# A chunked two-way recurrence on one core: inverting 64x64 diagonal blocks instead of 128x128 ones, with the next step's matrices built inside this step

## What is computed

```python
def _rwkv_step(S, xs):
    r, w, k, v, kk, a = xs
    sa = jnp.einsum('bhij,bhj->bhi', S, -kk)
    S = S * w[:, :, None, :] + sa[..., None] * (kk * a)[:, :, None, :] + v[..., None] * k[:, :, None, :]
    return S, jnp.einsum('bhij,bhj->bhi', S, r)
# forward and backward:
s, ys = lax.scan(_rwkv_step, s0.astype(f32), xs, reverse=reverse)
```

## Time and profile before

| | |
|---|---|
| median of 3 runs | 3408.24 us (3405.17 to 3410.75) |
| the profiled execution | 3406.34 us, span 3404.5 us |
| TensorE passes busy | 2853.8 us (84%), x16786 |
| VectorE, ScalarE, GpSimd busy | 1727.5, 1490.8, 334.1 us |
| HBM read | 458.30 MB |

### The profile page before, as it was taken

How to read it: one execution, slowest core, us unless ns; L and a number is a source line. 1 busy time by engine, 2 the same in 40 slices (tenths; PEclk the granted TensorE clock), 3 DMA queues, 4 the chain that set the end, 5 groups by cost and what they waited for, 6 DMA issues and landing times. The chain is left out here.

```text
span 3404.5 us, 47820 instructions
## 1 busy us (share of the span) xinstructions
PE 2853.8 (84%) x16786; PEld 2435.6 (72%) x16786; DVE 1727.5 (51%) x2453; ACT 1490.8 (44%) x2103; POOL 334.1 (10%) x469
## 2 busy tenths in 40 slices
PE   4994948888998767999896968997499999999994
PEld 2971937777787256888685848885488888888883
DVE  3135634444443424332223117873288888888886
ACT  1221744433433012333112215652177777777774
POOL 0024111111200010000010003311100000000002
PEclk7996969999999887999997988998599999999997
DMA  5233010000001522221313241112299999999996
GB/s 190 78 122 111 1 45 1 1 1 1 1 1 46 190 87 81 74 74 49 101 48 99 80 150 28 28 42 76 100 345 346 343 363 342 355 355 344 358 344 225
DMA packets 306607, 479.05 MB, mean 141 GB/s; under 512 B 58336, under 2 KB 228816, under 8 KB 306224
## 3 DMA queue, kind: packets, MB, share of 16 engines
q1 hardware_dynamic: 294912, 444.77, 38.6%
q10 hardware_dynamic: 7152, 17.89, 1.4%
q0 software_dynamic: 4416, 14.70, 1.3%
HBM read 458.30 MB, written 18.98 MB: 140 GB/s over the span
## 5 line engine op out<-in xcount | busy, mean ns | idle before, releaser
L2467 DVE TENSOR_TENSOR m_lo<-m_raw,m_hi 128x1408 fp32r<-128x1408 f32 (+1 forms) x459 | 662.7, 1462 | 140.1 <-ACT m_hi L2419 136.7
L2419 ACT ACTIVATE m_hi<-m_raw 128x1408 fp32r<-128x1408 f32 (+1 forms) x459 | 567.4, 1248 | 131.0 <-PE p_ups L2370 79.2
L186 PE MATMUL acc<-w_hi,h_hi 128*128 128x512 f32 (+1 forms) x1120 | 427.0, 381 | 41.8 <-DVE w_lo L171 35.8
L171 DVE TENSOR_TENSOR w_lo<-w_raw,w_hi 128x1024 fp32r<-128x1024 f32 (+1 forms) x134 | 157.8, 1179 | 561.0 <-ACT w_hi L164 560.9
L187 PE MATMUL acc<-w_lo,h_hi 128*128 128x512 f32 (+1 forms) x1120 | 425.5, 380 | 0.0
L188 PE MATMUL acc<-w_hi,h_lo 128*128 128x512 f32 (+1 forms) x1120 | 423.9, 378 | 0.0
L164 ACT ACTIVATE w_hi<-w_raw 128x1024 fp32r<-128x1024 f32 (+1 forms) x134 | 135.6, 1013 | 516.2 <-PE acc L188 480.5
L186 PEld LDWEIGHTS acc<-w_hi,h_hi 128*128 128x128 f32 x1120 | 212.9, 190 | 78.9 <-DVE w_lo L171 37.4
L188 PEld LDWEIGHTS acc<-w_hi,h_lo 128*128 128x128 f32 x1120 | 212.7, 190 | 34.3
L187 PEld LDWEIGHTS acc<-w_lo,h_hi 128*128 128x128 f32 x1120 | 213.0, 190 | 32.7
L1813 ACT ACTIVATE a_power<-p_unit 128x512 f32<-128x512 f32 x240 | 133.2, 561 | 205.7 <-PE p_unit L1737 205.7
(11 more groups left out here) (310 smaller groups left out, 5648.8 us busy)
## 6 DMA issues: line engine op xcount, KB each, us to landing
m_raw<-moe_w_gu SPq DMA_DIRECT2D x544, 352.0 KB
m_raw<-moe_w_dn SPq DMA_DIRECT2D x187, 512.0 KB
ada_w<-ada_w SPq DMA_DIRECT2D x40, 1024.0 KB, 8.2
w_raw<-ffn_w_gu SPq DMA_DIRECT2D x88, 256.0 KB, 2.9
w_raw<-w_in_o SPq DMA_DIRECT2D x24, 512.0 KB, 3.7
w_raw<-ffn_w_dn SPq DMA_DIRECT2D x22, 512.0 KB, 3.5
w_raw<-w_in_e SPq DMA_DIRECT2D x28, 384.0 KB, 3.3
scratch_y_slots<-y_slot ACTq DMA_DIRECT2D x18, 512.0 KB, 6.3
```

What stands on the lines that cost most here:

```text
L171: eng.tensor_tensor(self.w_lo[:, part, 0:2 * self.width], self.raw[:, slot, 0:2 * self.width], self.w_hi[:, part, 0:2 * self.width], ALU.s ...
L186: eng.matmul(out, hi, whi[:, b, :], start=first, stop=False)
L2419: a.activation(whi[:, u % MSPLIT, 0:size(u)], raw[:, s, 0:size(u)], ACT.Copy).then_inc(s_hi.sem, 1)
L2467: dve.tensor_tensor(wlo[:, u % MSPLIT, 0:n], raw[:, u % MRAW, 0:n], whi[:, u % MSPLIT, 0:n], ALU.subtract).then_inc(s_lo.sem, 1)
```

## The change

The 128x128 triangular matrix A of a head is split into 64x64 blocks. Only the two diagonal blocks are inverted by squaring, now with five squarings (levels 0 to 4) and five inverse products (levels 1 to 5), each a pair of 64x64 products in the two diagonal quarters of the array. The corner block follows from them: corner_pe (slots 6 and 7) multiplies the corner of A with one diagonal inverse, turns the other inverse, and multiplies the two, with a copy by ScalarE between and one by VectorE behind. TF is cleared once, so its other corner stays zero.

A step has eight slots (SLOTS_OF_STEP). walk puts products, masks and turns of step n + 1 into slots 4 to 6 of step n; chain_r, chain_u and chain_end go behind slots 0, 1 and 3. PREP has new slots, and each of its matrix products is two pieces in slots of their own. The PSUM banks are dealt anew: powers one bank a direction, one bank for the inverse products of both directions, two for the masked products, one for all turned matrices and preparation products. wait_read makes TensorE wait, before it writes a shared bank, until the last reader is done.

```diff
-    LEVELS = 6
+    LEVELS, SLOTS_OF_STEP = 6, 8
...
-            X = K.sb(scan, "a_power", [P, 2, 2, 2, 2, P])
-            W = K.sb(scan, "inverse_so_far", [P, 2, 2, 2, P])
+            AX = K.sb(scan, "a_turned", [P, 2, 2, 2, P])
+            XW = K.sb(scan, "powers_inverse", [P, 2, 2, 2, 3, HD])
             TF = K.sb(scan, "inverse_t", [P, 2, 2, 2, P])
+            PT = K.sb(scan, "inverse_parts", [P, 2, 2, 2, HD])
...
-            pU = [K.ps(scan, f"p_unit{d}", [P, 3, 512]) for d in range(2)]
+            pA = [K.ps(scan, f"p_powers{d}", [P, 512]) for d in range(2)]
+            pI = K.ps(scan, "p_inverse", [P, 512])
+            pM = K.ps(scan, "p_products", [P, 2, 512])
+            pX = K.ps(scan, "p_turned", [P, 512])
...
+            reader = {"turned": None, "inverse": None}
+            def wait_read(pe, bank, signal, count):
+                if reader[bank] is not None:
+                    pe.wait_ge(reader[bank][0].sem, reader[bank][0].at(reader[bank][1]))
+                reader[bank] = signal, count
+            def pair_pe(pe, ct, k, i, lhs, rhs):
+                a, b = PIECES[i]
+                if k == 0:
+                    wait_read(pe, "turned", s_eps, 2 * ct + i + 1)
+                else:
+                    wait_read(pe, "turned", s_sig, 8 * ct + 2 * (k - 1) + i + 1)
+                pe.matmul(pX[:, 0:b - a], lhs, rhs[:, a:b], start=True, stop=True).then_inc(s_prod.sem, 1)
...
+            PREP = [(0, "act", squares_act)] + [(1 + i, who, f(i)) for i in range(2) for who, f in (("pe", norm_pe), ("act", norm_act))]
+            PREP += [(3, "dve", norm_dve)]
+            for d, at in ((0, 4), (1, 19)):
+                PREP += [(at + 2 * w + i, who, f(d, w, i)) for w in range(2) for i in range(2) for who, f in (("pe", lora_pe), ("act", lora_act))]
+                PREP += [(at + 2, "pool", decay_pool(d)), (at + 4, "dve", scan_dve(d)), (at + 5, "dve", centre_dve(d)),
+                         (at + 5, "pool", rate_pool(d)), (at + 6, "pool", other_pool(d)),
+                         (at + 6, "act", middle_act(d)), (at + 8, "act", exps_act(d)), (at + 11, "dve", tilde_dve(d))]
...
-                if s:
-                    pe.wait_ge(u_tt[d].sem, u_tt[d].at(LEVELS * s))
-                pX, pM = pU[d][:, 2, :], pU[d][:, 0:2, :]
-                pairs = [k for k in range(5) if PAIR_STEP[k] < i] if ct + 1 < CT else []
-                last, k = (ct + 1, pairs[-1]) if pairs else (ct, 4)
-                if k == 0:
-                    pe.wait_ge(s_eps.sem, s_eps.at(2 * last + 2))
-                else:
-                    pe.wait_ge(s_sig.sem, s_sig.at(8 * last + 2 * k))
-                pe.transpose(pX[:, 2 * P:3 * P], cols(Kt[ct % 2][d], c), K.ident[:])
-                pe.transpose(pX[:, 3 * P:4 * P], cols(Bt[ct % 2][d], c), K.ident[:]).then_inc(u_xk.sem, 1)
+                wait_read(pe, "turned", u_kb, q + 1)
+                pe.transpose(pX[:, 0:P], cols(Kt[ct % 2][d], c), K.ident[:])
+                pe.transpose(pX[:, P:2 * P], cols(Bt[ct % 2][d], c), K.ident[:]).then_inc(u_xk.sem, 1)
+                if q:
+                    pe.wait_ge(u_rest.sem, u_rest.at(2 * q))
...
+                wait_read(pe, "turned", u_x0, q + 1)
...
+            def powers_bank(d):
+                return pA[d][:, 0:2 * P].rearrange("p (h x n) -> p h x n", h=2, x=2)
+            def inverse_bank():
+                return pI[:, 0:P].rearrange("p (h n) -> p h n", h=2)
             def level_pe(pe, ct, i, d, l):
                 q, s, c, par = unit(ct, i, d)
-                pA, pI = pU[d][:, 0, :], pU[d][:, 1, :]
+                if l >= LEVELS:
+                    return corner_pe(pe, ct, i, d, l)
+                cur, out = l % 2, powers_bank(d)
+                def x(hh, b):
+                    return AX[head(b), par, d, hh, head(b)] if l == 0 else XW[head(b), cur, d, hh, 2, :]
+                def xt(hh, b):
+                    return AM[head(b), par, d, hh, head(b)] if l == 0 else XW[head(b), cur, d, hh, 0, :]
                 if l == 0:
                     pe.wait_ge(u_x0.sem, u_x0.at(q + 1))
-                    pe.wait_ge(u_rest.sem, u_rest.at(2 * q + 2))
                 else:
-                    pe.wait_ge(u_xw[d].sem, u_xw[d].at(LEVELS * s + l))
-                cur = l % 2
-                if l < LEVELS:
+                    pe.wait_ge(u_xw[d].sem, u_xw[d].at((LEVELS - 1) * s + l))
+                if l < LEVELS - 1:
                     for hh in range(2):
-                        x = X[:, cur, d, hh, 1, :]
-                        xt = AM[:, par, d, hh, 0:P] if l == 0 else X[:, cur, d, hh, 0, :]
-                        if l < LEVELS - 1:
-                            pe.matmul(pA[:, 2 * hh * P:(2 * hh + 1) * P], x, xt, start=True, stop=True)
-                        mm = pe.matmul(pA[:, (2 * hh + 1) * P:(2 * hh + 2) * P], xt, x, start=True, stop=True)
+                        if l < LEVELS - 2:
+                            for b in range(2):
+                                pe.matmul(out[head(b), hh, 0, :], x(hh, b), xt(hh, b), start=True, stop=True)
+                        for b in range(2):
+                            mm = pe.matmul(out[head(b), hh, 1, :], xt(hh, b), x(hh, b), start=True, stop=True)
                     mm.then_inc(u_sq[d].sem, 1)
                 if l:
                     if l == 1:
-                        pe.wait_ge(u_tt0.sem, u_tt0.at(q + 1))
+                        pe.wait_ge(u_tt0.sem, u_tt0.at(2 * q + 2))
                     else:
                         pe.wait_ge(u_tt[d].sem, u_tt[d].at(LEVELS * s + l - 1))
+                    wait_read(pe, "inverse", u_tt[d], LEVELS * s + l + (l == LEVELS - 1))
                     for hh in range(2):
-                        mm = pe.matmul(pI[:, hh * P:(hh + 1) * P], X[:, cur, d, hh, 1, :], W[:, cur, d, hh, :], start=True, stop=True)
+                        for b in range(2):
+                            mm = pe.matmul(inverse_bank()[head(b), hh, :], x(hh, b), XW[head(b), cur, d, hh, 1, :], start=True, stop=True)
                     mm.then_inc(u_iv[d].sem, 1)
+            def corner_pe(pe, ct, i, d, l):
+                q, s, c, par = unit(ct, i, d)
+                near, far = head(d), head(1 - d)
+                if l == LEVELS:
+                    pe.wait_ge(u_tt[d].sem, u_tt[d].at(LEVELS * (s + 1)))
+                    for hh in range(2):
+                        pe.matmul(pA[d][near, hh * HD:(hh + 1) * HD], AX[far, par, d, hh, near], TF[far, par, d, hh, far], start=True, stop=True)
+                    for hh in range(2):
+                        mm = pe.matmul(pA[d][near, P + hh * HD:P + (hh + 1) * HD], TF[:, par, d, hh, near], K.ident[:, near], start=True, stop=True)
+                    mm.then_inc(u_ab[d].sem, 1)
+                else:
+                    pe.wait_ge(u_pt[d].sem, u_pt[d].at(s + 1))
+                    wait_read(pe, "inverse", u_fin[d], s + 1)
+                    for hh in range(2):
+                        mm = pe.matmul(pI[near, hh * HD:(hh + 1) * HD], PT[near, d, 1, hh, :], PT[near, d, 0, hh, :], start=True, stop=True)
+                    mm.then_inc(u_c[d].sem, 1)
...
-                pe.wait_ge(u_tt[d].sem, u_tt[d].at(LEVELS * (s + 1)))
+                pe.wait_ge(u_fin[d].sem, u_fin[d].at(s + 1))
...
-                a.wait_ge(u_sq[d].sem, u_sq[d].at(LEVELS * s + l + 1))
-                if l:
-                    a.wait_ge(u_iv[d].sem, u_iv[d].at(LEVELS * s + l - 1))
                 if l < LEVELS - 1:
-                    out, src = X[:, (l + 1) % 2, d].rearrange("p h x n -> p (h x n)"), pU[d][:, 0, :]
-                else:
-                    out, src = X[:, (l + 1) % 2, d, :, 1, :], pU[d][:, 0, :].rearrange("p (h x n) -> p h x n", h=2, x=2)[:, :, 1, :]
-                a.activation(out, src, ACT.Copy).then_inc(u_xw[d].sem, 1)
+                    a.wait_ge(u_sq[d].sem, u_sq[d].at((LEVELS - 1) * s + l + 1))
+                    first = 0 if l < LEVELS - 2 else 1
+                    a.activation(XW[:, (l + 1) % 2, d, :, 2 * first::2, :], powers_bank(d)[:, :, first:, :], ACT.Copy).then_inc(u_xw[d].sem, 1)
+                elif l == LEVELS:
+                    near = head(d)
+                    a.wait_ge(u_ab[d].sem, u_ab[d].at(s + 1))
+                    a.activation(PT[near, d].rearrange("p x h n -> p (x h n)"), pA[d][near, 0:2 * P], ACT.Copy).then_inc(u_pt[d].sem, 1)
...
+                if l < LEVELS - 1:
+                    dve.tensor_tensor(XW[:, (l + 1) % 2, d, :, 1, :], XW[:, l % 2, d, :, 1, :], inverse_bank(), ALU.add).then_inc(u_tt[d].sem, 1)
+                elif l == LEVELS - 1:
+                    if q >= 4:
+                        dve.wait_ge(c_y.sem, c_y.at(q - 3))
+                    for b in range(2):
+                        dve.tensor_tensor(TF[head(b), par, d, :, head(b)], XW[head(b), l % 2, d, :, 1, :], inverse_bank()[head(b)],
+                                          ALU.add).then_inc(u_tt[d].sem, 1)
+                elif l == LEVELS + 1:
```

(35 more changed lines are left out.)

## The result

The changed kernel takes 3435.62 us (median of 5 runs, 3434.13 to 3448.35) against 3410.75 for the kernel before on the same chip: ratio 1.0081, 95% interval 1.006 to 1.0102. It is slower by 0.8%, where 0.9% faster was forecast. The time is inside the range given, its sign was the unlikely one. The span of the profiled execution is 3434.1 us, 29.6 longer than before.

A forecast was written before the change was run, and what follows sets the result against it. TensorE was taken to bound the recurrence. Quiet steps of 21.9 against 24.92 us save 60 us in 20 steps; preparation costs 27 and the first pair 4, leaving about 30 us faster: 3378 us, range 3330 to 3440.

The forecast's parts named there:

- Passes and their number: Levels on TensorE: 16 squaring and 8 inverse passes of 29 ns, 0.70 us a direction and level instead of 1.34.
- Rival 1: Levels: diagonal tiles take turns on one bank, 58 ns a pass, step 26.7 us, time 3465 us; chance 0.17.
- Shared bank and the wait behind the masks: Inverse products 0.93 us apart; level 5 of direction 1 waits 2.3 us behind VectorE's masks, 0.6 of it filled.
- Shape changes: TensorE switching tile shape: about 14 more changes a step, taken at 0.15 us each.
- the sum of a quiet step: TensorE's step without preparation, from one last product pass of direction 0 to the next: 21.9 us against 24.92.
- Rival 3: Quiet steps: shape changes nearly free and overlapped by waits, 28 us less, time 3350 us; chance 0.14.
- One sign: VectorE's busy share in a quiet step would rise from 10.3 in 24.9 us to half.
- rival 2: Every step: the clock falls to half for 3.4 us, costing up to 1.7 us, time 3412 us; chance 0.13.
- Preparation: Steps preparing the next pair of heads: some 9 us dearer a pair than 26.3, 27 us in three pairs.
- the second scan: Preparing steps: TensorE idle 1.8 us while VectorE's second scan stands in front of a needed addition.
- the second set of matrices: Preparing steps: TensorE idle 1.9 us while VectorE makes the second set of scaled matrices.
- The start: First pair's preparation, before the recurrence: no cover, its pieces take turns on the bank, 4 us dearer.

The follow-up runs named there:

- the wide passes in slot 6: Changed kernel, idle 1.68 us kept, with seven 128x128 products put in front of direction 0's corner products: 3425.01 us.
- among whole matrices: Kernel before, with three spare VectorE products ahead of direction 0's level 5 addition in the last five steps: 3417.55 us (544 columns), 3421.97 us (640).
- at level 3: Changed kernel with level 5 products in their direction's own bank, plus spare 640-column VectorE products ahead of direction 0's level 3 addition, last five steps: 3396.54 us.
- the order alone: Changed kernel's walk and shared banks, but whole 128x128 squarings and inverse products with seven levels as in the kernel before: 3430.77 us, ratio 1.0075.
- the blocks alone: Changed kernel's 64x64 blocks and corners, but each step's products, masks and turns at its own start as before: 3486.26 us, ratio 1.0227.

## Why the prediction was wrong

**Passes and their number: right.** 29 ns a 64x64 pass, both diagonal tiles on one bank at once (1047.38 to 1047.49). Rival 1, tiles in turn, is refuted. The two tiles lie on different rows of the array and write one bank, and here the measurement decides against the rule cited with it. They write different partitions of it, and no row shown has two row tiles on the same ones.

**Shared bank and the wait behind the masks: right.** Inverse products follow at 0.92 us (1049.53 and 1050.45) for 0.93, and the idle ahead of level 5 of direction 1 is 1.68 us for 2.3 less 0.6.

**Shape changes and the sum of a quiet step: right at full clock.** 21.9 us was forecast; the kernels whose only difference is work inside the idle have 21.83 and 21.92, where the step of before has 24.92. Rival 3 falls with it. One sign was off: VectorE is busy 9.2 us of such a step, 0.42 of it, where half was forecast. And chain_u stands in the sum with 0.90 us where its row reads 0.84.

**The clock: the step that failed.** "A quiet step of after" was summed at clock 1.00, and rival 2 priced a fall at 3.4 us of half speed a step, from the one short fall in the earlier trace rows, with a chance of 0.13. A fall came in each of the five quiet steps. In four it lasted 13.7 us and cost 5.5 us a step instead of 1.7 at most; in the fourth step it lasted 3.4 and cost 1.5, the rival's price. In the whole recurrence the granted clock is 0.77, so about 284 of 617.6 us ran at half speed; before it was 0.94, some 71 of 593. The mechanism of the rival was right, its size was off by three, and it took the place of the forecast. The price was read from one of the shortest falls of the kernel before; others there lasted 6.8 us (as 597.65 to 604.47).

The recurrence took 55 us more than forecast (617.6 against some 563). 23.5 of them are in the five quiet steps (133.0, from 972.80 to 1105.80, against 109.5), some 31 in the fifteen preparing ones. That the time lies inside the range is luck: the range reached up to 3440 to hold the case of one short fall a step, and what came were falls four times as long.

**Preparation: mis-sized, for the same reason.** Two of the idle places came as forecast, 5.23 us at the reciprocal for 5.5 and 2.98 at the first set of scaled matrices for 2.9:

```profile
849.18 0.58 PE L1763 MATMUL p_inverse<-powers_inverse 64*64 64x64 f32 x6 [5.23 <-DVE powers_inverse L1883]
...
898.32 0.55 PE L1791 MATMUL p_chain<-v_rows,a_masked 128*128 128x64 f32 x3 [2.98 <-DVE state_mid L1905]
```

Others did not: the second scan left 4.28 us (925.91 to 930.19) for 1.8, the second set of matrices no more than a quiet step has for 1.9. Their sum is near the forecast: TensorE is idle 27.0 of the 152.9 us, 14.6 more than in five slow quiet steps, for 14. But a pair's preparation costs 45.8 us over quiet steps where these run at full clock (148.60 less five of 20.57), not 35. In that kernel the clock is 0.79 over the five steps, so 31 us of full speed are missing (0.21 of 148.6); before, at 0.94 of 150.9, it was 9. The sum had left this term at what it was before. In the changed kernel itself preparation looks cheap, 152.9 against five quiet steps' 133.0, only because the quiet steps are slow too. The start was forecast 4 us dearer and is 2.7 later.

**What stays open.** That the idle 1.68 us brings the falls of the quiet steps is shown: with the wait gone, or with passes in its place, they run at clock 1.00. When an idle brings a fall, and how long it lasts, is not settled. The fourth quiet step has the same passes and the same idle as the others, and a fall of 3.4 us. In the first four the falls start 1.30, 1.21, 1.12 and 1.01 us behind the idle: they come 27.3 us apart, the steps are 27.4 us long. So the moment at which the idle comes is a rival to what stands behind it, and it was not tested: no run moves one and keeps the other. With it agrees that of five like idles only some had a fall behind them, one beside the wide passes in slot 6, two among whole matrices, two at level 3, three in the order alone. If the stretch behind the idle has a part in it, the turns are not enough, since in the order alone they follow the idle and the falls stayed at 3.4 us. And the blocks alone fall deepest with no idle over 0.84 us; whether their six short ones add up, or the passes between them count, is open.

## What to carry to other kernels

Before work on TensorE is made smaller, list the idle places that its other engines will open, and read the granted clock as a term of the sum: here 1.7 us of idle cost 6.8 in four of five quiet steps. A fall may be priced too low from the shortest one in sight. A shared PSUM bank made such a place here, because its reader stood in a queue behind other work; giving the one product that waits a bank that is free at that moment turned 0.8% slower into 0.8% faster. Cutting the element-wise pieces that stand in front of a short step gave 29 us here (3381.04 to 3352.04); do it before the step is shortened.

## What the runs showed of the hardware

- Two 64x64 tiles on the diagonal with outputs in one bank run together at 29 ns a float32 pass with 64 columns.
- Idle of 0.72 us a step: no fall. Idle of 1.40 us among whole matrices: none in three steps; 1.70: a fall of 3.4 us behind two of five. Idle of 1.68 with the products, turns and corners behind it: a fall of 13.7 us in four of five steps, clock 0.75, and of 3.4 in one, 0.93; the same with 14 wide passes 2.1 us behind it: one fall of 3.4 in five steps, clock 1.00 and 0.96. Six idles of 0.3 to 0.84 us a step with 64x64 passes between: clock 0.67.
- In the changed kernel the falls of the quiet steps start 1.0 to 1.5 us after the end of the idle 1.68.
- 56 small passes in the idle held the clock at 1.00 as 14 wide ones did.
